# Product-key experts in a two-block model: two dense passes over the expert tables in place of gathered rows

## The chip, the cores and the metric

One core of a Trainium2 chip runs the whole program. The metric is the device time of one execution in microseconds (us); less is better.

## The reference

The input is x with 256 tokens of 1024 features, float32 throughout. A first model of two layers (recurrence, latent attention, memory attention, output projection, layer norm) is followed by one block of a second model (dilated attention and a pooling mixer, then the experts). Only the experts change:

```python
def peer_ffn(h, w_q, sub_keys, expert_u, expert_v):    # 8 heads, 2 x 128 sub-keys, top 16
    q = einsum('cd,de->ce', xc, w_q).reshape(C, 8, 2, 128)
    s = einsum('chpk,pnk->chpn', q, sub_keys)
    sv, si = top_k(s, 16)
    cand = sv[:, :, 0, :, None] + sv[:, :, 1, None, :]           # 256 sums
    cand_id = si[:, :, 0, :, None] * 128 + si[:, :, 1, None, :]
    top_v, top_pos = top_k(cand, 16)
    gate = softmax(top_v)
    u = expert_u[eid]; act = gelu(einsum('cd,chkd->chk', xc, u))
    vv = expert_v[eid]
    y = einsum('chk,chkd->cd', gate * act, vv)
```

So each token picks 8 x 16 = 128 of 16384 experts. An expert is one row of 1024 values in each of two tables of 67 MB. The block ends with x + g2 * y and an RMS norm.

## The kernel before, in words

Five engines run queues that are written out by hand. For each block a string (PE_ORDER, ACT_LAST, DVE_LAST) lists tasks, and each engine's loop at the end of its function turns a task name into instructions. Engines meet at semaphores. Nothing is planned by a scheduler: what stands behind a wait on its engine waits too.

**The tiles.** The 256 tokens are two tiles, t (0 to 127) and u (128 to 255). Weights come in units of 128 x 4096 float32 (2.1 MB) through a ring of three slots, which SP (SyncE's queue) refills as units are used up. PSUM is two tiles `pj` of 1024 columns and four banks of 512.

**The last block, up to the experts.** Scores (S), weights (P), values (Y) and the output product (O, line 775) give x; Zt and Zu turn the normed tiles (line 699) into `xT`. K0 to K3 are the units of w_q; `expert_queries` (line 1021) makes queries of them, `sub_key_scores` (line 1040, tasks E) the scores against the sub-keys, and VectorE's `route` (line 1854, tasks Rt0 to Rt7, Ru0 to Ru7) finds the top 16 of a head. K1 and K2 do not lie in the ring but in tiles that are free by then. `chosen` (line 1930) makes expert numbers of the picks with comparisons against an iota (lines 1942 to 1949).

**The experts.** Pick n = (tile, j) of 256 takes four steps. GpSimd's queue issues an indirect DMA (line 674) that gathers, for 128 tokens, one row of the joined table (u and v side by side, 2048 values) into one of 16 row slots of 1.05 MB. VectorE multiplies the u half with the token and sums it (`dots_of`, line 1993). ScalarE (`expert_weights`, lines 1407 to 1415) takes gelu, the gate, and writes a diagonal 128 x 128 matrix of the weights. TensorE multiplies that matrix with the v half, two products of 512 columns (line 1173, and 1187 for the last two picks), and sums over the picks in PSUM. A slot is gathered into again once its products are done. Tasks `D<n>` and `W<n>` say how far VectorE, ScalarE and TensorE go before the next task of another kind; picks of tile t run while queries and routes of tile u are still being made. `Ra` (line 1913) is a shortcut to the first eight picks. `Ht` and `Hu` turn the tile back into token rows for the dots.

**The end.** `end_sums` (lines 2005 to 2009) and `finish` (line 2016) add the sums to x and norm the tile; SP stores it.

Of the kernel before, what the change touches and what calls it, by code (L numbers as in the profile page):

```python
# [38 lines left out]
ROWS = PICKS * TT  # L39
GROUP = 4  # L40
N_SLOTS = 15
EARLY_SLOT, EARLY_UNTIL = N_SLOTS, 24
N_DIAG = 8
N_SPLIT = 2
# [24 lines left out]
            K0at Y3 E0t P5 Y4 Y5 Ht O1w O0v O0w K0bt W1 W2 E1t W3 W5 W6 W8 K1at K1bt W11 W14 W16 Zu W18 E2t W19 K1au W20  # L69
            W22 E3t K0au W23 W24 W25 K0bu K1bu W26 EU0 W27 W28 W29 W30 W31 Hu K20 W32 K21 W33 W35 W36 W37 W41 K22 W42  # L70
            W44 W45 K23 EU1 W46 W47 W48 W49 E4 E5 W50 K30 W51 W53 K31 W55 W56 K32 K33 W58 E6 W60 W65 W66 W67 W68 W69 E7
            W256"""]
# [4 lines left out]
ACT_LAST = """Xu BU BK BQa BQb SK S0 S1 MT S2 BV P0 P1 S3 S4 P2 S5 OMta OMtb P3 Zt K0at P4 P5 E0t Ht T1 W3 K0bt W5 W6 W7 W8  # L77
    E1t W9 OMu W10 W12 K1bt W13 W14 W15 W16 T2 W17 W18 Zu W19 W20 E2t W22 E3t W24 W25 K0bu W26 W27 W28 W29 W30 W31
    EU0 T3 K1bu W32 W33 W35 Hu W38 W39 W40 W41 W43 W44 W47 W48 W49 EU1 W50 W51 K23 E4 W52 E5 W53 W54 W56 W57 K33 W58
    W59 W60 T4 W61 W63 W64 E6 W65 W69 W70 W71 E7 W73 W78 W79 T5 W102 T6 W130 T7 W148 FN0 W256 FN1"""  # L80
# [4 lines left out]
DVE_LAST = """Xu S0 S1 S2 PL0 PL1 N0 N1 S3 N2 S4 S5 N3 N4 Y1 N5 OMt NMt Zt Ra Y5 Rt0 XP1 GT1 D1 D3 D6 OMu D7 D8 D9 Rt1 D10 D11  # L85
    D12 XP2 D14 D16 NMu D17 GT2 D19 D20 Zu D21 D23 Rt2 D24 D25 Rt3 D27 XP3 D28 D31 D34 D36 GT3 D37 D45 D47 D51 D53
    D54 D55 Rt4 D56 Rt5 XP4 D57 D60 D61 D68 Rt6 GT4 D69 D70 D72 D73 Rt7 D74 D75 D76 D78 D79 D80 XP5 GT5 D81 D83 D85
    Ru0 D88 Ru1 D92 Ru2 D96 Ru3 D100 XP6 D108 GT6 D110 Ru4 D114 Ru5 D118 Ru6 D122 Ru7 D126 XP7 D136 GT7 D140 FS0
    D156 FN0 D256 FS1 FN1"""


def pe_tasks():

    out, loads, pieces = [], 0, 0
    for text in PE_ORDER:
        tasks = []
        for task in text.split():
# [92 lines left out]
def bank_uses(l, task):  # L190

    if task in ("Xt", "Xu", "Zt", "Zu", "Ht", "Hu"):
# [5 lines left out]
    if task[0] == "E":  # L198
        return [(task,)]
    if l == B2 and task[0] == "Y":  # L200
# [31 lines left out]
def bank_index():  # L232
# [28 lines left out]
def picks_order():  # L261

    free, out, last = [], [], {}
    for n in range(ROWS):
        if n in NEW_SLOTS:
            free = list(NEW_SLOTS[n][1]) + free
        if n >= EARLY_UNTIL and EARLY_SLOT in free:
            free.remove(EARLY_SLOT)
        k = free.pop(0)
        out.append((k, last.get(k), sum(1 for q in out if q[0] == k)))  # L270
        last[k] = n
        free.append(k)
    return out


NEW_SLOTS = {0: ('', (6, 15, 2, 3, 4, 5, 7, 8)), 32: ('K1', (0, 1)), 56: ('K2', (9, 10)), 67: ('K3', (11, 12, 13)), 186: ('E7', (14,))}


def constants():
# [20 lines left out]
    for d in (4, 16):  # L300
# [13 lines left out]
        "c_iota": np.arange(16, dtype=np.float32).reshape(1, 16),  # L314
# [3 lines left out]
def build(nc, d, out):  # L318
# [9 lines left out]
    PICK = picks_order()  # L328

    with ExitStack() as ctx:  # L330
# [11 lines left out]
        more_rows = sb("more_rows", [P, 2, D_MODEL])  # L342
# [29 lines left out]
        sm = sb("sm", [P, 2, TT, T])
        pT = sb("pT", [P, 2, TT, T])
# [6 lines left out]
        flat_pair, far_pair = flat_tri[:, 0:D_MODEL], flat_tri[:, D_MODEL:].rearrange("p (h t) -> p h t", t=P)  # L380
# [21 lines left out]
        def flat(tile):  # L402
# [3 lines left out]

        shape5 = dict(t=TT, h=PEER_HEADS, two=2)
# [5 lines left out]
        top_val = flat(rstd)[:, 0:PICKS * TT].rearrange("p (t h k) -> p t h k", t=TT, h=PEER_HEADS)  # L413
        gate = flat(rstd)[:, PICKS * TT:].rearrange("p (t j) -> p t j", t=TT)
        skT = flat(sq)[:, 512:768].rearrange("p (a k) -> p a k", a=2)
        cand, cand_left = flat(sq)[:, 0:256], flat(sq)[:, 256:512]
        first_of, second_of = flat(vM)[:, 0:PICKS], flat(vM)[:, PICKS:2 * PICKS]
        id_a, id_b = flat(vM)[:, 2 * PICKS:3 * PICKS], flat(vM)[:, 3 * PICKS:4 * PICKS]
        expert = flat(vM)[:, 512:768].bitcast(u32).rearrange("p (t j) -> p t j", t=TT)
        dots = flat(vM)[:, 768:1024].rearrange("p (t j) -> p t j", t=TT)  # L420
        onehot = flat(qT).rearrange("p (j i) -> p j i", i=TOPK)

        ring_rows = [[ring[:, UNIT[B2, unit] % RING, g * 2 * D_MODEL:(g + 1) * 2 * D_MODEL] for g in range(2)]
                     for unit in ("K1", "K2", "K3")]
        flat_y = flat(yT)
        aside = [flat(b), flat_y[:, 2 * D_MODEL:]]
        spare_rows = [flat(more_rows), flat(kM)]
        row_slot = ([flat(more_rows), flat(kM), flat(qvE), flat(qM)] + ring_rows[1] + [flat(hv)]
                    + ring_rows[0] + aside + ring_rows[2] + [flat(xT), flat_y[:, 0:2 * D_MODEL], flat(kT)])
        assert len(row_slot) == N_SLOTS + 1  # L430
        diag = [far_pair[:, g, :] for g in range(4)] + [causal[:, g // 2, (g % 2) * P:(g % 2 + 1) * P] for g in range(4)]
        assert len(diag) == N_DIAG
        acts, weights_of = rope[:, 0, :], rope[:, 1, :]
        first_scores = [sm[:, i // 2, i % 2, :] for i in range(4)] + [pT[:, i // 2, i % 2, :] for i in range(4)]
# [46 lines left out]
        SPLIT_OF = {name: n for n, name in enumerate(t for t in TASKS[B2] if t in ("K0at", "K0bt", "K1bt"))}  # L481
        QUERY_OF = {name: n for n, name in enumerate(t for t in ACT_LAST.split() if t[0] == "K")}
# [30 lines left out]
        N_B2 = 5  # L513
# [5 lines left out]
        def _(sp):  # L519
# [12 lines left out]
            def weights(n):  # L532
# [41 lines left out]

            for l in range(DEPTH + 1):
                units = [name for k, name in LOADS if k == l]
                for name in units:
# [18 lines left out]
                    if name == units[3] and l == B2:  # L596
# [4 lines left out]
                        for row, c in ((row_gate1, 2), (row_gate2, 5)):  # L601
                            load(row, mod_rows[c * DC:(c + 1) * DC, :].rearrange("(o c) p -> o (c p)", o=1)
                                 .to_broadcast([P, D_MODEL]), "mod_rows_load")
                    if name == units[2] and l == B2:
# [5 lines left out]
                        load(final_g, d["final_g_2"].rearrange("(o n) -> o n", o=1).to_broadcast([P, D_MODEL]), "b2_load")  # L610
# [1555 lines left out]
```

## Time and profile before

| what | value |
|---|---|
| median of 3 runs | 1395.61 us (1394.95 to 1398.93) |
| the profiled execution: span from first to last instruction | 1393.4 us |
| TensorE busy | 1274.3 us (91%) |
| VectorE busy | 813.1 us (58%) |
| GpSimd busy | 653.1 us (47%) |
| ScalarE busy | 436.1 us (31%) |
| moved by DMA | 406.77 MB |

A busy TensorE holds the latency of its last matmuls too, so its share is more than what it computes; the distance from one matmul to the next is read from stretches in which it never waits. The span is the profiled execution's own time; the median of the runs is 2.2 us more.

### The profile page before, as it was taken

Reading aid. Unit: us, or ns where it says so; the run is one execution under the profiler, and the core shown is the slowest. Engines: PE = TensorE matmul, PEld = TensorE weight load, DVE = VectorE, ACT = ScalarE, POOL = GpSimd, SP = SyncE. Lnnn points to the kernel's source line nnn. Section 1 sums busy time; section 2 is a strip of 40 time slices with the busy share of each in tenths; the row PEclk is TensorE's granted clock in tenths of the full one; section 3 lists DMA queues with packets and bytes.
Section 4 is the critical chain, followed back from the end, with each engine's and each line's share of the span. In section 5 each row is a group of like instructions: output and inputs, shape, how many; then the busy total and the mean of one; then the engine's idle time right before and its main releaser. Section 6 shows DMA issues by size and latency. Waiting matters only on the chain.

```text
span 1393.4 us, 17185 instructions
## 1 busy us (share of the span) xinstructions
PE 1274.3 (91%) x6328; PEld 785.6 (56%) x6328; DVE 813.1 (58%) x1694; ACT 436.1 (31%) x1065; POOL 653.1 (47%) x647
## 2 busy tenths in 40 slices
PE   9999999999999999999999999989677887877886
PEld 8887686648886686549655565633232333323332
DVE  1776377441666387352357764879888654444445
ACT  1533344111334334212334433243323232222223
POOL 0556667431636667422104444455533645554540
PEclk9999999999999999999999999999998989998999
DMA  9544335546444344635449999999999999999995
GB/s 374 213 167 173 131 125 209 210 157 222 152 170 179 122 167 170 254 137 208 172 171 412 420 406 421 419 419 421 422 421 421 421 423 421 422 421 422 422 421 240
DMA packets 54061, 406.77 MB, mean 292 GB/s; under 512 B 6213, under 2 KB 8666, under 8 KB 11610
## 3 DMA queue, kind: packets, MB, share of 16 engines
q0 software_dynamic: 37184, 268.45, 46.5%
q1 hardware_dynamic: 15706, 136.18, 25.3%
q10 hardware_dynamic: 1088, 1.05, 0.3%
q8 instruction: 50, 0.82, 0.2%
q14 instruction: 33, 0.27, 0.1%
HBM read 403.53 MB, written 1.07 MB: 290 GB/s over the span
## 4 chain that ended last, share of the span: by engine, by line
PE 33%; DMA 24%; DVE 6%; ACT 3%; issue 1%; POOL 0%; DVEq 0%; ACTq 0%
DMA ring<-in_peer_uv,vM 12%; PE bank L1173 11%; PE pj L739 6%; PE pj L775 6%; DMA qM<-in_peer_uv,vM 5%; DMA xT<-in_peer_uv,vM 4%; PE pj L1036 3%; PE pj L754 3%; DMA more_rows<-in_peer_uv,vM 2%; DMA b<-in_peer_uv,vM 2%; DVE ring L1993 1%; ACT rope L1409 1%; PE bank L699 1%; DVE qM L1993 0%; PE bank L1046 0%
## 5 line engine op out<-in xcount | busy, mean ns | idle before, releaser
L739 PE MATMUL pj<-xT,ring 128*128 128x256 f32 (+1 forms) x1568 | 318.4, 363 | 0.9 <-ACT hv L1343 0.4
L739 PEld LDWEIGHTS pj<-xT,ring 128*128 128x128 f32 x1568 | 276.6, 190 | 36.5 <-issue 2.6
L674 POOL DMA_INDIRECT ring<-in_peer_uv,vM x108 | 129.8, 1202 | 124.1 <-PE bank L1173 108.2
L635 POOL TENSOR_SCALAR more_rows<-more_rows,lbt 128x256 f32<-128x256 f32 x168 | 175.7, 1046 | 16.4
L1993 DVE SCALAR_TENSOR_TENSOR ring<-ring,memT 128x1024 f32<-128x1024 f32 x110 | 133.6, 1224 | 83.9 <-DMA ring<-in_peer_uv,vM 83.2
L1407 ACT ACTIVATE rope<-vM 128x1 f32<-128x1 f32 (+2 forms) x112 | 22.6, 202 | 385.1 <-DVE ring L1993 166.1
L1173 PE MATMUL bank<-ring,causal 128*128 128x512 f32 x256 | 123.5, 629 | 20.2 <-ACT causal L1415 20.2
L775 PE MATMUL pj<-ring,yT 128*128 128x512 f32 x320 | 140.8, 594 | 0.0
L633 POOL TENSOR_SCALAR mod_part<-more_rows,lbt 128x256 f32<-128x256 f32 x24 | 22.8, 951 | 245.7 <-issue 121.3
L636 POOL TENSOR_TENSOR mod_part<-mod_part,more_rows 128x256 f32<-128x256 f32 x168 | 128.4, 765 | 14.0
L1173 PE MATMUL bank<-ring,tri 128*128 128x512 f32 x176 | 84.8, 624 | 18.5 <-ACT tri L1415 18.4
L1173 PEld LDWEIGHTS bank<-ring,causal 128*128 128x128 f32 x256 | 51.2, 203 | 88.1 <-issue 61.4
L775 PEld LDWEIGHTS pj<-ring,yT 128*128 128x128 f32 x320 | 59.8, 190 | 69.8 <-issue 69.5
L1173 PEld LDWEIGHTS bank<-ring,tri 128*128 128x128 f32 x176 | 34.0, 199 | 65.4 <-issue 38.8
L754 PE MATMUL pj<-ring,xT 128*128 128x512 f32 x160 | 70.5, 595 | 0.0
L674 POOL DMA_INDIRECT hv<-in_peer_uv,vM x21 | 25.4, 1211 | 94.8 <-DVE vM L1952 68.2
L1409 ACT ACTIVATE rope<-rope,rstd 128x1 f32<-128x1 f32 x256 | 59.6, 285 | 3.6
L1739 DVE COPY_PREDICATED tri<-level_mask,bank 128x512 f32<-128x512 uint8 x56 | 41.0, 733 | 21.4 <-PE bank L879 19.2
L754 PEld LDWEIGHTS pj<-ring,xT 128*128 128x128 f32 x160 | 29.8, 190 | 34.8 <-issue 34.4
L1305 ACT ACTIVATE big<-big 128x1024 f32<-128x1024 f32 x32 | 34.3, 1073 | 40.3 <-DVE big L1710 23.1
L1415 ACT ACTIVATE causal<-eye,rope 128x128 f32<-128x128 f32 x128 | 44.2, 393 | 1.8
L674 POOL DMA_INDIRECT qM<-in_peer_uv,vM x21 | 24.9, 1184 | 42.3 <-PE bank L1173 34.0
(386 smaller groups left out, 2053.0 us busy)
## 6 DMA issues: line engine op xcount, KB each, us to landing
ring<-in_units SPq DMA_DIRECT2D x43, 2048.0 KB, 9.5
more_rows<-in_w_ada SPq DMA_DIRECT2D x24, 1024.0 KB, 4.9
ring<-in_units SPq DMA_DIRECT2D x2, 1536.0 KB, 8.0
ring<-in_peer_uv,vM POOLq DMA_INDIRECT x108, 21.4
memT<-in_mem SPq DMA_DIRECT2D x2, 512.0 KB, 5.3
ring<-in_units SPq DMA_DIRECT2D x1, 1024.0 KB, 8.9
xT<-in_x_turned SPq DMA_DIRECT2D x1, 1024.0 KB, 10.8
x<-in_x SPq DMA_DIRECT2D x1, 1024.0 KB, 16.3
```

Of the source, the lines that this page charges most:

```text
L635: do(g.tensor_scalar(mod_w[:, c, :], mod_w[:, c, :], silu_c[:, c:c + 1], None, ALU.mult))
L636: do(g.tensor_tensor(part, part, mod_w[:, c, :], ALU.add), "mod_partial" if c == DC - 1 else None)
L674: pool.indirect_dma_start(row_slot[k], None, d["peer_uv_2"], bass.IndirectOffsetOnAxis(ap=expert[:, t, j:j + 1], axis=0))\
L739: ins = nc.tensor.matmul(pj[s][0:n, 2 * m + first:2 * m + stop], ring[:, slot, at:at + n], act[:, c, first:stop], start=(c == 0), stop=(c ...
L754: ins = nc.tensor.matmul(pj[s][:, t * COLS:(t + 1) * COLS], act[:, c, t * P:(t + 1) * P], w[:, c, :], start=(c == 0), stop=(c == DC - 1))
L775: ins = nc.tensor.matmul(pj[t][:, n * 512:(n + 1) * 512], yT[:, 4 * j + c, t * P:(t + 1) * P], w[:, c, n * 512:(n + 1) * 512], start=(firs ...
L1036: ins = nc.tensor.matmul(pj[s][:, 2 * m * P + first:2 * m * P + stop], w[c][:, m * P:(m + 1) * P], xT[:, c, first:stop], start=(c == 0), s ...
L1173: ins = nc.tensor.matmul(bank[2 * (1 - t) + half][:, :], diag[n % N_DIAG], row_slot[PICK[n][0]][:, c0:c0 + COLS], start=(j == 0), stop=(j ...
L1409: a.activation(weights_of[:, n0 + k:n0 + k + 1], acts[:, n0 + k:n0 + k + 1], ACT.Copy, scale=gate[:, t, j + k:j + k + 1]).then_inc(sem("ro ...
L1415: a.activation(diag[n % N_DIAG], eye[:, :], ACT.Copy, scale=weights_of[:, n:n + 1])\
L1739: do(v.copy_predicated(dst, mask, B), *bank_free(key))
L1993: v.scalar_tensor_tensor(out=row_slot[k][:, 0:D_MODEL], in0=row_slot[k][:, 0:D_MODEL], scalar=1.0, in1=normed[:, t, :], op0=ALU.mult, op1= ...
```

## The change

The gathered rows go away. Both tables are now read whole, for all 256 tokens, in three stages after the queries:

- **A0 to A63** (`pair_products`). A unit of the u table holds 4 of the 128 second keys for all 128 first keys. One task takes two second keys and makes 2 x 8 products of 256 columns: the dots of 256 experts with all tokens. ScalarE's gelu moves each result into `act_all`, a tile of 128 first keys x (128 second keys x 256 tokens). It lies over most of the tiles of the earlier blocks, which are now laid by hand.
- **B0 to B31** (`hot_rows`, `gated`, `batch_gates`, `batch_weights`). Tasks J0 and J1 turn the picks (first key, second key, gate) so that picks lie on partitions. For 8 tokens at a time VectorE compares them with an iota (two one-hot tiles of 128 x 1024), GpSimd multiplies one of them by the gates, TensorE makes one 128 x 128 product per token, whose entry is the gate of that pair of keys (0 where it was not picked), and VectorE multiplies it into `act_all`.
- **V0 to V31** (`value_sums`). A unit of the v table holds 4 second keys; per key, 2 tiles and 2 halves, one product of 512 columns. The first three and the last three units take the tiles apart.

Queries run tile by tile, `K<i>t` then `K<i>u`, into four halves of `pj`. `Ra`, `Ht`, `Hu`, `dots_of`, `expert_weights` and the split gathers of the last two picks are gone; `chosen` leaves first and second keys as numbers in `picks`. SP loads 64 more units. The rows of gate 2 and of the final norm are loaded late, into `xT`.

The diff, cut to its core:

```diff
-            """... K0at Y3 E0t P5 Y4 Y5 Ht O1w O0v O0w K0bt W1 W2 E1t W3 W5 W6 W8 K1at K1bt W11 ... W69 E7
-            W256"""]
+            """... K0t Y3 E0t P5 Y4 Y5 O1w O0v O0w K1t K2t E1t Zu K3t E2t K0u E3t K1u E0u K2u E1u K3u E2u A0 E3u A1 A2 A3 A4 A5
+            A6 A7 A8 A9 A10 A11 A12 A13 J0 A14 ... A29 J1 A30 A31
+            AB V0t V1t V2t V0u V1u V2u VV V29t V30t V31t V29ua V30ua V31ua V29ub V30ub V31ub"""]
...
+    both = " ".join([f"A{k}" for k in range(32, PAIRS)] + [f"B{i}" for i in range(BATCHES)])
...
-DVE_LAST = """... Y5 Rt0 XP1 GT1 D1 D3 D6 OMu D7 D8 D9 Rt1 ... D256 FS1 FN1"""
+DVE_LAST = """... Y5 Rt0 OMu NMu Zu Rt1 Rt2 Rt3 Rt4 Rt5 Rt6 Rt7
+    CEt CHt GTt Ru0 Ru1 Ru2 Ru3 Ru4 Ru5 Ru6 Ru7 CEu CHu GTu HM FS0 FN0 FS1 FN1"""
...
+            for n in range(2 * EXPERT_UNITS):
+                r = FIRST_EXPERT + n
+                ring_released(sp, r)
+                src = (d["peer_u_2"][n] if n < EXPERT_UNITS else
+                       d["peer_v_2"][:, (n - EXPERT_UNITS) * DC * COLS:(n - EXPERT_UNITS + 1) * DC * COLS])
+                load(ring[:, r % RING, :], src, f"ring_load{r % RING}")
...
-                    pool.indirect_dma_start(row_slot[k], None, d["peer_uv_2"],
-                                            bass.IndirectOffsetOnAxis(ap=expert[:, t, j:j + 1], axis=0))\
-                        .then_inc(sem(f"row_load{k}"), 16)
...
+            def gated(i):
+
+                pool.wait_ge(sem("hot_made"), 2 * (i + 1))
+                seconds = hot[:, i % 2, 1, :, :]
+                do(g.tensor_tensor(seconds, seconds, picks_turned[:, 2, i * BATCH:(i + 1) * BATCH].unsqueeze(2)
+                                   .to_broadcast([P, BATCH, NKEYS]), ALU.mult), "hot_ready")
...
+            def pair_products(task):
+
+                k, n = int(task[1:]), HALF[task]
+                slot = ring_loaded(pe, FIRST_EXPERT + k // 2)
+                half_empty(pe, n)
+                for i in range(2):
+                    for c in range(DC):
+                        at = (2 * (k % 2) + i) * D_MODEL + c * P
+                        ins = nc.tensor.matmul(half_bank[n % 4][:, i * T:(i + 1) * T], ring[:, slot, at:at + P], xT[:, c, :],
+                                               start=(c == 0), stop=(c == DC - 1))
+                last(ins, "half_filled")
+
+            def batch_gates(i):
+
+                pe.wait_ge(sem("hot_ready"), i + 1)
+                for q in range(2):
+                    key = (l, ("B", i, q))
+                    bank_empty(pe, key)
+                    for n in range(4):
+                        ins = nc.tensor.matmul(bank_of(key)[:, n * P:(n + 1) * P], hot[:, i % 2, 0, 4 * q + n, :],
+                                               hot[:, i % 2, 1, 4 * q + n, :], start=True, stop=True)
+                    last(ins)
...
+                for at in range(4):
+                    k = 4 * n + at
+                    for t in tiles:
+                        for half in halves:
...
+                            ins = nc.tensor.matmul(half_bank[2 * t + half], act_all[:, k, t * P:(t + 1) * P],
+                                                   ring[:, slot, at * D_MODEL + half * COLS:at * D_MODEL + (half + 1) * COLS],
+                                                   start=(k == 0), stop=(k == NKEYS - 1))
...
+                do(a.activation(act_all[:, 2 * k:2 * k + 2, :], half_bank[n % 4].rearrange("p (a t) -> p a t", a=2), ACT.Gelu),
...
-                    v.scalar_tensor_tensor(out=row_slot[k][:, 0:D_MODEL], in0=row_slot[k][:, 0:D_MODEL], scalar=1.0,
-                                           in1=normed[:, t, :], op0=ALU.mult, op1=ALU.mult,
-                                           accum_out=dots[:, t, j:j + 1]).then_inc(sem("dot_done"), 1)
...
+            def hot_rows(i):
+
+                if i >= 2:
+                    bank_filled(dve, (l, ("B", i - 2, 1)))
+                dve.wait_ge(sem("picks_turned"), i * BATCH // P + 1)
+                for k in range(2):
+                    v.tensor_tensor(hot[:, i % 2, k, :, :], iota[:, :].unsqueeze(1).to_broadcast([P, BATCH, NKEYS]),
+                                    picks_turned[:, k, i * BATCH:(i + 1) * BATCH].unsqueeze(2).to_broadcast([P, BATCH, NKEYS]),
+                                    ALU.is_equal).then_inc(sem("hot_made"), 1)
+
+            def batch_weights(i):
+
+                dve.wait_ge(sem("acts_kept"), PAIRS)
+                for q in range(2):
+                    key = (l, ("B", i, q))
+                    bank_filled(dve, key)
+                    t0 = i * BATCH + 4 * q
+                    weights = act_all[:, :, t0:t0 + 4]
+                    v.tensor_tensor(weights, bank_of(key)[:, :].rearrange("p (t n) -> p n t", t=4), weights,
+                                    ALU.mult).then_inc(sem(bank_free(key)[0]), 1)
...
+                elif name == "HM":
+                    hot_rows(0)
+                    for i in range(BATCHES):
+                        if i + 1 < BATCHES:
+                            hot_rows(i + 1)
+                        batch_weights(i)
...
-    arrays["peer_uv_2"] = np.concatenate([arrays.pop("peer_u_2")[0], arrays.pop("peer_v_2")[0]], axis=1)
+    arrays["peer_u_2"] = np.ascontiguousarray(arrays["peer_u_2"][0].reshape(NKEYS, EXPERT_UNITS, 4, DC, P).transpose(1, 4, 2, 3, 0)
+                                              .reshape(EXPERT_UNITS, P, DC * COLS))
+    arrays["peer_v_2"] = arrays["peer_v_2"][0].reshape(NKEYS, NKEYS * D_MODEL)
```

**How the order moves.** TensorE, before, from the last transposes ahead of the experts on (L699 with xT is Ht, L775 the last output product, L1036 queries, L1046 sub-key scores, L1173 the picks' products):

```order
L1130 MATMUL bank<-qM,qvE 64x128 x8
L699 MATMUL bank<-eye,xT 128x128 x8
L775 MATMUL pj<-ring,yT 128x512 x12
L1036 MATMUL pj<-xT,ring 128x128 x16
L1173 MATMUL bank<-hv,tri 128x512 x2
L1173 MATMUL bank<-kT,tri 128x512 x2
L1046 MATMUL bank<-sq,yT 128x128 x2
```

TensorE, changed, the same place up to K1t, and then the whole of it from K3u to the end (L756 is the output product, L1017 queries, L1029 sub-key scores, L682 transposes, L1041 `pair_products`, L1052 `batch_gates`, L1065 `value_sums`):

```order
L1151 MATMUL bank<-qM,qvE 64x128 x8
L756 MATMUL pj<-ring,yT 128x512 x12
L1017 MATMUL pj<-xT,more_rows 128x128 x4
...
L1017 MATMUL pj<-xT,ring 128x128 x32
L1029 MATMUL bank<-sq,yT 128x128 x4
L1041 MATMUL pj<-xT,ring 128x256 x16
L1029 MATMUL bank<-sq,yT 128x128 x4
L1041 MATMUL pj<-xT,ring 128x256 x208
L682 MATMUL bank<-eye,yT 128x128 x3
...
L1041 MATMUL pj<-xT,ring 128x256 x544
L1052 MATMUL bank<-hot 128x128 x256
L1065 MATMUL pj<-ring,act_all 128x512 x512
```

All queries, scores and 1024 pair products now stand ahead of the first product of the gates, and all 256 of those ahead of the first sum over values; nothing is interleaved any more but two transposes.

VectorE, before, near its end (L1993 is a dot):

```order
L1993 SCALAR_TENSOR_TENSOR xT,vM<-xT,memT 128x1024
L1993 SCALAR_TENSOR_TENSOR b,vM<-b,memT 128x1024
L1993 SCALAR_TENSOR_TENSOR yT,vM<-yT,memT 128x1024
L1603 TENSOR_SCALAR stat<-stat 128x1
L2016 TENSOR_SCALAR x<-pT,stat 128x512 x2
```

VectorE, changed, from the last gates (L1873) to the end (L1882 is `hot_rows`, L1894 `batch_weights`, L1904 and L1905 `end_sums`):

```order
L1873 TENSOR_TENSOR yT<-rstd,stat 128x128
L1882 TENSOR_TENSOR hot<-iota,vM 128x1024 x4
L1894 TENSOR_TENSOR act_all<-bank,act_all 128x128x4 x2
L1882 TENSOR_TENSOR hot<-iota,vM 128x1024 x2
L1894 TENSOR_TENSOR act_all<-bank,act_all 128x128x4 x2
...
L1882 TENSOR_TENSOR hot<-iota,vM 128x1024 x2
L1894 TENSOR_TENSOR act_all<-bank,act_all 128x128x4 x4
L1904 TENSOR_TENSOR hot<-pj,xT 128x512
```

The 256 dots are gone, and 64 comparisons and 64 small products alternate, two and two. GpSimd, which had the gathers, has 32 rows `L668 TENSOR_TENSOR hot<-hot,vM 128x1024` in their place.

## Rows read from the trace of the kernel before

**Rows 1.** The page: span, busy time by engine, GB/s in 40 equal slices, gathers' queue

```profile
span 1393.4 us, 17185 instructions
PE 1274.3 (91%) x6328; PEld 785.6 (56%) x6328; DVE 813.1 (58%) x1694; ACT 436.1 (31%) x1065; POOL 653.1 (47%) x647
...
GB/s 374 213 167 173 131 125 209 210 157 222 152 170 179 122 167 170 254 137 208 172 171 412 420 406 421 419 419 421 422 421 421 421 423 421 422 421 422 422 421 240
...
q0 software_dynamic: 37184, 268.45, 46.5%
```

**Rows 2.** Windows: start:end, length, busy of the engines, PEclk, DMA share, GB/s

```profile
500.00:600.00 100.00, 99.83 (x787) 66.05 (x786) 60.91 (x91) 30.36 (x46) 64.92 (x72) 1.00 0.52 203
1000.00:1100.00 100.00, 73.86 (x153) 30.73 (x152) 83.09 (x216) 28.98 (x96) 46.81 (x39) 0.90 1.01 421
```

**Rows 3.** Chain that ended last: start us, us, what it was

```profile
1225.62 2.00 PE bank L1173 x4
...
1227.88 24.70 DMA more_rows<-in_peer_uv,vM
...
1252.61 1.24 DVE more_rows L1993 x2
```

**Rows 4.** Timeline of TensorE: start us, us, line, operation, count, [idle before it]

```profile
725.98 1.09 PE L699 MATMUL bank<-eye,xT 128*128 128x128 f32 x8
726.91 10.47 PE L775 MATMUL pj<-ring,yT 128*128 128x512 f32 x24
737.21 3.73 PE L1036 MATMUL pj<-xT,ring 128*128 128x128 f32 x32
742.23 1.96 PE L1173 MATMUL bank<-hv,tri 128*128 128x512 f32 x4 [1.29 <-ACT tri L1415]
...
1205.76 2.84 PE L1173 MATMUL bank<-ring,causal 128*128 128x512 f32 x4 [2.81 <-ACT causal L1415]
```

**Rows 5.** Chain, TensorE never waiting: products of 256, 512, 128 and 128 columns

```profile
545.91 13.81 PE pj L739 x64
703.78 6.88 PE pj L775 x16
805.03 7.14 PE pj L1036 x64
865.88 0.89 PE bank L1046 x8
```

**Rows 6.** Timeline of VectorE: first and last row of one route; one-hot comparisons

```profile
756.84 0.48 DVE L1869 MAX8 cT<-sm 128x8 f32<-128x128 f32 x2
...
761.03 0.42 DVE L1911 FIND_INDEX8 kE<-rstd,sq 128x8 uint32<-128x256 f32 x1
...
1058.54 2.36 DVE L1942 TENSOR_TENSOR qT<-mod_part,vM 128x1024 f32<-128x1024 f32 x2
```

**Rows 7.** Groups of GpSimd by form: count, busy us and mean ns, idle before

```profile
L647 POOL TENSOR_TENSOR b<-kT,b 128x1024 f32<-128x1024 f32 x1 | 2.4, 2352 | 0.1
```

**Rows 8.** Timeline of all engines, 136 to 141: start us, us, engine, line

```profile
136.36 0.93 POOL L635 TENSOR_SCALAR more_rows<-more_rows,lbt 128x256 f32<-128x256 f32 x1
136.41 0.69 DVE L1781 SCALAR_TENSOR_TENSOR sm<-bank,causal 128x512 f32<-128x512 f32 x1 [0.21 <-DVE tri L1739]
...
137.13 0.59 ACT L1249 COPY pT<-bank 128x512 f32<-128x512 f32 x1 [2.35 <-PE bank L699]
...
139.21 0.73 POOL L636 TENSOR_TENSOR mod_part<-mod_part,more_rows 128x256 f32<-128x256 f32 x1
...
139.39 1.09 DVE L1668 TENSOR_TENSOR sm<-sm,stat 128x512 f32<-128x512 f32 x1
```

**Rows 9.** Windows as in rows 2, around a pause of TensorE

```profile
1208.00:1210.00 2.00, 2.00 (x3) 0.66 (x2) 1.12 (x2) 0.00 (x0) 1.05 (x1) 0.50 0.99 414
1210.00:1212.00 2.00, 2.00 (x6) 0.94 (x5) 1.23 (x2) 0.00 (x0) 0.57 (x1) 0.96 1.01 422
```

**Rows 10.** Chain as in rows 3, its last products

```profile
1382.45 3.45 PE bank L1187 x8
```

More of the change, by code:

```diff
@@ L68 @@
             """Xt BUt BKt Xu MT BUu BKu BQa BQb SK S0 S1 BVa S2 PL0 PL1 BVb P0 P1 S3 S4 Y0 S5 Y1 O1t P2 O0t P3 O1v Zt Y2 P4
-            K0at Y3 E0t P5 Y4 Y5 Ht O1w O0v O0w K0bt W1 W2 E1t W3 W5 W6 W8 K1at K1bt W11 W14 W16 Zu W18 E2t W19 K1au W20
-            W22 E3t K0au W23 W24 W25 K0bu K1bu W26 EU0 W27 W28 W29 W30 W31 Hu K20 W32 K21 W33 W35 W36 W37 W41 K22 W42
-            W44 W45 K23 EU1 W46 W47 W48 W49 E4 E5 W50 K30 W51 W53 K31 W55 W56 K32 K33 W58 E6 W60 W65 W66 W67 W68 W69 E7
-            W256"""]
+            K0t Y3 E0t P5 Y4 Y5 O1w O0v O0w K1t K2t E1t Zu K3t E2t K0u E3t K1u E0u K2u E1u K3u E2u A0 E3u A1 A2 A3 A4 A5
+            A6 A7 A8 A9 A10 A11 A12 A13 J0 A14 A15 A16 A17 A18 A19 A20 A21 A22 A23 A24 A25 A26 A27 A28 A29 J1 A30 A31
+            AB V0t V1t V2t V0u V1u V2u VV V29t V30t V31t V29ua V30ua V31ua V29ub V30ub V31ub"""]
 ACT_HEAD = ["MK", "X MK"]
@@ L76 @@
     Le18 HO2 HN2 HO3 HN3 LN"""
[L77 to L80, printed above, removed]
+ACT_LAST = """Xu BU BK BQa BQb SK S0 S1 MT S2 BV P0 P1 S3 S4 P2 S5 OMta OMtb P3 Zt P4 K0t E0t P5 OMua OMub K1t K2t E1t
+    Zu K3t E2t K0u E3t K1u E0u K2u E1u K3u E2u A0 E3u A1 A2 A3 A4 A5 A6 A7 A8 A9 A10 T0 A11 A12 A13 J0 A14 A15 A16 A17
+    A18 A19 A20 A21 A22 A23 A24 A25 A26 T1 A27 A28 A29 J1 A30 A31 AB FN0 FN1"""
 DVE_ORDER = """F0 N FP0 R0 R1 R2 R3 Da01 KR Da02 S0 Db01 P0 Db02 L01 S1 Da03 L02 AD Db03 Da04 F1 AD S2 Da05 L03 Da06
@@ L197, in bank_uses @@
         return [("MT",)]
-    if task[0] == "E":
+    if task[0] in "EJ":
         return [(task,)]
+    if task[0] == "B" and task[1:].isdigit():
+        return [("B", int(task[1:]), q) for q in range(2)]
     if l == B2 and task[0] == "Y":
@@ L258, in bank_index @@
     return out, uses
[L261 to L276, printed above, removed]
+HALF = {task: n for n, task in enumerate(
+    [t for t in TASKS[B2] if t[0] == "K"] + [t for t in TASKS[B2] if t[0] == "A" and t[1:].isdigit()])}
+ASIDE = [UNIT[B2, "K1"], UNIT[B2, "K2"]]
+RING_UNITS = [n for n in range(len(STREAM)) if n not in ASIDE]
+RING_AT = {n: r for r, n in enumerate(RING_UNITS)}
+FIRST_EXPERT = len(RING_UNITS)
 def constants():
@@ L419, in build @@
[L419 to L426, printed above, removed]
-        spare_rows = [flat(more_rows), flat(kM)]
@@ L428, in build @@
[L428 to L434, printed above, removed]
@@ L1019, in _, with expert_queries @@
             l = B2
-            def expert_queries(name, columns, tiles):
+            def expert_queries(task):
+                name, t = task[:2], "tu".index(task[2])
                 if name in ("K1", "K2"):
@@ L1038, in expert_queries @@
-                return ins
-            def sub_key_scores(key, ready, products):
+                n = HALF[task]
+                half_empty(pe, n)
+                after(pe, "xT_ready", l - 1, 2 * t + 5)
+                for m in range(4):
+                    for c in range(DC):
+                        ins = nc.tensor.matmul(half_bank[n % 4][:, m * P:(m + 1) * P], w[c][:, m * P:(m + 1) * P],
+                                               xT[:, c, t * P:(t + 1) * P], start=(c == 0), stop=(c == DC - 1))
```

565 lines of the change are left out of this document (208 added, 357 removed).

## The prediction, made before the changed kernel ran

> **What bounds the kernel now.** The page comes first: TensorE is busy for 91% of the span, and 268 MB, two thirds of all bytes, pass through the gathers' queue [rows 1]. The slices of GB/s then cut the kernel in two. For 21 slices, some 735 us, the DMA moves 122 to 254 GB/s after the start; for the 18 slices from there on it moves 406 to 423 [rows 1]. The windows say which limit holds in each part. From 500 to 600 TensorE is busy for 99.8 us of 100 at granted clock 1.00; from 1000 to 1100 for 73.9, while the 16 DMA engines are at 1.01 of their time [rows 2]. The chain of waits shows the cycle of the second part: two products in 2.00 us, the next gather into the slot they free, 24.7 us, a dot of 1.24 [rows 3]; gelu and diagonal on ScalarE lie between a dot and its products. So the first part is bound by TensorE, and the second, some 650 us, by 268 MB at 421 GB/s, that is 638 us. TensorE's work in it is hidden.
>
> One thing about the counts decides everything below. In the program a pick takes two products of 512 columns; in the timeline it is x4 [rows 4], and the 12 output products of O1w, O0v and O0w are x24 [rows 4]. A float32 product leaves **two records**, two passes of the array. Only transposes leave one (8 for Ht, x8) [rows 4].
>
> The prices of a record where TensorE never waits [rows 5]: 256 columns 13.81 / 64 = 0.2158 us; 512 columns 6.88 / 16 = 0.430 us; 128 columns 7.14 / 64 = 0.1116 us, and 0.89 / 8 = 0.111 us for a score.
>
> **The change, step by step.** Off goes the whole second part as it is, gathers, dots, diagonals and their slots. What takes its place has one order on TensorE, so I add it up in time.
>
> *Up to the end of the output product.* The two first models do not change on any engine. O0w ended at 737.2 [rows 4]. Ahead of it Ht goes (8 transposes, 0.93 by the distance of its start to the next row's [rows 4]), K0t has 32 products in place of 16 (+32 records, 3.57) and E0t 4 in place of 2 (+4 records, 0.45). End: 740.3.
>
> *Queries.* K1t, K2t, K3t and K0u to K3u are 7 tasks of 64 records, 7 x 7.14 = 50.0 us. Six tasks E of 8 records are 5.3, Zu 0.9. A0 begins at 796.5. Does TensorE wait here? Zu needs gate 1, two adds, the norm and ScalarE's sums for tile u; K1t, K2t and E1t give these 15 us, and a route (4.6 us from first to last row [rows 6]) ahead of them on VectorE is over by then. I take 0.
>
> *Stage A.* 64 tasks x 16 products x 2 records = 2048 x 0.2158 = **442.0 us**; E3u and the transposes J0, J1 within it are 1.6. A unit of 2.1 MB feeds 13.8 us of products, and at 421 GB/s [rows 1] it takes 5.0, so SP's loads are hidden. ScalarE has 6.9 us for each result of 512 columns; a copy of one took 0.59 [rows 8]. VectorE's routes are hidden too: 16 x 4.6 = 74 us, and for each tile 12 comparisons, multiplications and sums of 1024 elements at 1.15 (two took 2.36, of which some 0.07 is latency that overlaps what follows) [rows 6], some 16 with the rest, all over about 80 us after A0 begins, where J1 stands 30 tasks, 207 us, behind it. If that cover were gone the cost would be its excess over 207. End of A: 1240.1.
>
> *Stage B.* This is where the trace before shows no such work. Batches 0 and 1 are ready in advance, but the first `batch_weights` waits for the last gelu, and only its end lets the third pair of one-hot tiles start. Per batch: two comparisons of 128 x 1024, 2.29 [rows 6]; one GpSimd product of 128 x 1024, 2.35 [rows 7]; 16 records of 128 columns, 1.8; two small products of 128 x 512 from PSUM, 0.69 each, 1.4 [rows 8]. Whether the first two overlap decides. At 139.39 a VectorE product with both inputs in SBUF began while GpSimd's ran until 139.94, and took 1.09 us; it ended 0.54 after GpSimd's. One of the same shape with an input in PSUM took 0.69 beside a GpSimd instruction of 0.93 [rows 8]. So comparisons and gate products take turns, and the small products lie under GpSimd's. The round is 2.29 + 2.35 + 0.1 for the hand-over = 4.74 us. The ends: with no exclusion the round is VectorE's alone, 2.29 + 1.4 = 3.7; with GpSimd at the rate of its 256 columns, 4 x 0.73 = 2.92 [rows 8], it is 5.3; with the small products exposed as well, since their reads step through memory as no row before does, 6.1 or more. I take 4.74, as the rows of full width are the nearest. From the end of A: 1.1 until the first bank is filled, 1.4, 30 rounds = 142.2, and the last batch's 1.8 on TensorE: **146.5 us**. The sums over values begin at 1386.6.
>
> *Stage V.* 128 keys x 2 tiles x 2 halves = 512 products, 1024 records x 0.430 = **440.3 us**. These are as many products as the picks had, but now nothing hides them. The clock: after a pause of 2.81 us [rows 4] TensorE was at 0.50, the 1.2 GHz level, for the 2 us from 1208, and at 0.96 in the 2 us after them [rows 9]. In B it pauses 3 us in each round. Slow gates stay under VectorE's comparisons; V then starts slow, which costs about 2 us once. V0t to V2t, 20 us, cover the last small products. A unit takes 13.8 us here as well, so its transfer is hidden down to 2.1 MB / 13.8 = 152 GB/s. End: 1828.9.
>
> The rows of the v table for one unit lie 512 KB apart, 16 KB in each. The Trainium skill, "DMA: Bandwidth & Descriptors", section "Latency and other measured facts", warns of row pitches at large powers of two: 207 GB/s for copies with a pitch of 512 KiB, 103 at 4 MiB. By 207 a unit would take 10.1 us and the sum stays; by 103 it would take 20.4 and V some 190 us more (29 of them and the start). No run here shows such a load.
>
> *The end.* From the last product to the end of the span was 1393.4 - 1385.9 = 7.5 us [rows 1, 10]; the same steps follow, and tile t's lie under tile u's products. Span: 1836.4. The median of the runs was 2.2 us above the profiled span, so the forecast is **1839 us**, 32% slower. In one sum: 650 us bound by transfers are traded for 59 + 442 + 147 + 440, bound by TensorE except in B.
>
> **The rivals.**
> *The passes are one* (this ends faster). Had a product one pass, as the transposes have, A would be 221, V 220, the queries 25 and the gates no less: 1839 - 221 - 220 - 27 = 1371 us. It decides below about 0.12 us for 256 columns. For it speaks only that the order lists 1024 and 512 products; against it the x24 for 12 and the x4 for two [rows 4]. 1%.
> *No exclusion in B.* If broadcast inputs do not take the port, the round is 3.7: 31 us less, 1808. For it: no row shows two broadcast inputs. Against: rows 8. 12%.
> *A longer round.* GpSimd at 2.92, or small products that outlast GpSimd's: 5.3 to 6.1 per round, 1856 to 1880. For it: the banks are read with a step of 128 values and `act_all` in pieces of 4. [...] 22%.
> *V waits for its units.* At 122 GB/s, the lowest slice [rows 1], a unit takes 17.2 us; 29 loads one after another and the start come to 540 in place of 440: 1939. It decides at 152 GB/s. Against: gathers of scattered 8 KB rows ran at 421 [rows 1]. 5%.
> *A lower clock in A or V.* At 0.90, as in 1000 to 1100 [rows 2], they would be 98 us longer, 1937. Against: 99.8% busy at 1.00 [rows 2]. 3%.
>
> **How the numbers follow.** The forecast has 57%, its own range 1825 to 1855. A measurement can tell 0.3%, some 4 us, from no change. All cases but the first rival are far slower: slower 0.99, faster 0.01, same 0. The range takes in both ends of the round in B and ends where slow loads or a slow clock begin: 1803 to 1882.
>
> **What would show it.** TensorE's distance of 0.216 us between records in A and 0.430 in V with no idle time; A0 near 797, the first gate product of stage B's flow near 1240, V near 1387. In B, comparisons that begin while GpSimd multiplies and take over 2 us in place of 1.15, and a round of 4.7 us. DMA at about 150 GB/s in A and V. Wrong would be: TensorE waiting for `ring` in V, a round under 4 or over 6, or a granted clock below 1.00 in the middle of A.

## The result and the profile after

The changed kernel takes **1825.09 us** (median; 1824.1 to 1826.28) against 1395.66 us before: a ratio of 1.3073, 95% interval 1.3054 to 1.3091. The forecast was 1839, with 1803 to 1882; its own range, 1825 to 1855, is met only at its lower edge.

The page of the changed kernel, to be laid beside [rows 1]. Row q1 is SP's queue, which now carries the tables; the last three rows are groups of instructions (count, busy us and mean ns of one, idle time before):

```profile
span 1824.0 us, 21425 instructions
PE 1757.2 (96%) x9006; PEld 1248.1 (68%) x9006; DVE 622.6 (34%) x1219; ACT 288.9 (16%) x481; POOL 404.6 (22%) x419
...
GB/s 333 204 144 127 197 179 193 193 187 139 132 216 197 177 90 228 105 127 139 151 172 139 143 172 147 139 162 69 1 0 63 191 163 160 138 157 165 138 153 55
...
q1 hardware_dynamic: 24922, 270.46, 38.3%
L1041 PE MATMUL pj<-xT,ring 128*128 128x256 f32 x2048 | 442.7, 379 | 0.0
L1065 PE MATMUL pj<-ring,act_all 128*128 128x512 f32 x1024 | 440.6, 593 | 0.0
L668 POOL TENSOR_TENSOR hot<-hot,vM 128x1024 f32<-128x1024 f32 x32 | 61.5, 1922 | 642.6 <-DVE hot L1882 642.6
```

All bytes went from 407 to 273 MB, and the 18 slices at over 400 GB/s are gone: no slice after the first exceeds 228. TensorE went from 91% to 96% busy. Lines 1041 and 1065 show what the forecast rests on: 1024 and 512 products, 2048 and 1024 records, and no idle time ahead of any of them. In the whole stretch from 790 to 1820 TensorE's only waits are these (us in total, times, longest):

```profile
PE bank L1052 <- POOL hot L668: 50.9, 30, 3.3
```

The chain that ended last, from the last queries on (start us, us, what):

```profile
789.23 7.15 PE pj L1017 x64
796.38 0.89 PE bank L1029 x8
797.27 6.91 PE pj L1041 x32
...
1006.03 234.83 PE pj L1041 x1088
1240.85 1.80 PE bank L1052 x16
...
1251.82 2.36 DVE hot L1882 x2
1254.32 1.91 POOL hot L668
1256.27 2.06 PE bank L1052 x16
1259.62 3.07 DVE hot L1882 x2
...
1376.06 440.43 PE pj L1065 x1024
```

One can lay this beside [rows 3]. Before, the long step of each cycle was a transfer of 24.7 us; now no transfer is in the chain from 797 on. The chain is TensorE for 443.6 us, then comparisons, gate products and TensorE by turns for 135.2 us, then TensorE for 440.4.

The windows of stages A, B and V, columns as in [rows 2], the granted clock third from the end:

```profile
1000.00:1240.00 240.00, 240.00 (x1115) 211.28 (x1114) 0.00 (x0) 20.78 (x35) 0.00 (x0) 1.00 0.40 149
1260.00:1380.00 120.00, 77.11 (x440) 68.74 (x441) 106.27 (x106) 0.00 (x0) 49.74 (x27) 0.79 0.00 1
1400.00:1600.00 200.00, 200.00 (x467) 88.54 (x466) 0.00 (x0) 0.00 (x0) 0.00 (x0) 1.00 0.43 166
```

A and V hold TensorE at full clock and everything else nearly idle. In B no engine is at its end: TensorE 64%, VectorE 89% (which holds the time that its comparisons are blocked), GpSimd 41%, and DMA nothing.

The turns in B, GpSimd and then VectorE of the changed kernel (start us, us, engine, line):

```profile
1319.33 1.90 POOL L668 TENSOR_TENSOR hot<-hot,vM 128x1024 f32<-128x1024 f32 x1 [2.72 <-DVE hot L1882]
...
1323.59 1.90 POOL L668 TENSOR_TENSOR hot<-hot,vM 128x1024 f32<-128x1024 f32 x1 [2.36 <-DVE hot L1882]
```

```profile
1316.83 2.35 DVE L1882 TENSOR_TENSOR hot<-iota,vM 128x1024 f32<-128x1024 f32 x2
1319.10 1.28 DVE L1894 TENSOR_TENSOR act_all<-bank,act_all 128x512 f32<-128x512 f32 x2
1320.30 3.14 DVE L1882 TENSOR_TENSOR hot<-iota,vM 128x1024 f32<-128x1024 f32 x2
1323.37 1.27 DVE L1894 TENSOR_TENSOR act_all<-bank,act_all 128x512 f32<-128x512 f32 x2
```

The two small products, 1.28 us, run at full speed under the gate product. The two comparisons that begin at 1320.30, while it still runs until 1321.23, take 3.14 us, in place of 2.35 for the two at 1316.83, which meet no gate product. So the one that is held takes some 1.9 us, a little under the "over 2 us" that was forecast. It is the pattern of [rows 8] at full size.

### The profile page after: what moved, and what is told of

Read it like the earlier page. It is cut to its first block, busy times and chain, and to the rows that moved or that the text cites. A ratio compares the mean times of both kernels' runs of the same rounds, so it can differ in the third digit from the quotient of the medians.

```text
span 1824.0 us, 21425 instructions
## 1 busy us (share of the span) xinstructions
PE 1757.2 (96%) x9006; PEld 1248.1 (68%) x9006; DVE 622.6 (34%) x1219; ACT 288.9 (16%) x481; POOL 404.6 (22%) x419
## 4 chain that ended last, share of the span: by engine, by line
PE 69%; DVE 3%; POOL 1%; issue 1%; ACT 0%; POOLq 0%; DVEq 0%; ACTq 0%
PE pj L1041 24%; PE pj L1065 24%; PE pj L720 5%; PE pj L756 4%; PE pj L1017 3%; PE bank L1052 2%; DVE hot L1882 2%; PE pj L735 2%; POOL hot L668 1%; PE bank L682 0%; DVE act_all L1894 0%; PE bank L1029 0%; PE bank L1151 0%; PE bank L860 0%; PE bank L792 0%
## 5 line engine op out<-in xcount | busy, mean ns | idle before, releaser
L1041 PE MATMUL pj<-xT,ring 128*128 128x256 f32 x2048 | 442.7, 379 | 0.0
L1065 PE MATMUL pj<-ring,act_all 128*128 128x512 f32 x1024 | 440.6, 593 | 0.0
L1041 PEld LDWEIGHTS pj<-xT,ring 128*128 128x128 f32 x2048 | 388.8, 190 | 52.7
L1065 PEld LDWEIGHTS pj<-ring,act_all 128*128 128x128 f32 x1024 | 195.0, 191 | 245.0 <-issue 245.0
L720 PEld LDWEIGHTS pj<-xT,ring 128*128 128x128 f32 x1568 | 276.6, 190 | 36.5 <-issue 2.6
L668 POOL TENSOR_TENSOR hot<-hot,vM 128x1024 f32<-128x1024 f32 x32 | 61.5, 1922 | 642.6 <-DVE hot L1882 642.6
L1904 DVE TENSOR_TENSOR hot<-pj,xT 128x512 f32<-128x512 f32 x4 | 2.8, 693 | 432.2 <-PE pj L1065 432.1
L756 PE MATMUL pj<-ring,yT 128*128 128x512 f32 x320 | 140.9, 595 | 0.0
L1052 PE MATMUL bank<-hot 128*128 128x128 f32 x512 | 84.5, 333 | 50.9 <-POOL hot L668 50.9
L1894 DVE TENSOR_TENSOR act_all<-bank,act_all 128x512 f32<-128x512 f32 x64 | 42.3, 683 | 258.6 <-PE bank L1052 258.2
L1052 PEld LDWEIGHTS bank<-hot 128*128 128x128 f32 x512 | 77.3, 239 | 58.0 <-POOL hot L668 57.9
L756 PEld LDWEIGHTS pj<-ring,yT 128*128 128x128 f32 x320 | 59.8, 190 | 69.9 <-issue 69.7
L1381 ACT ACTIVATE act_all<-pj 128x512 f32<-128x512 f32 x64 | 38.2, 597 | 386.7 <-PE pj L1041 386.6
L1882 DVE TENSOR_TENSOR hot<-iota,vM 128x1024 f32<-128x1024 f32 x64 | 91.8, 1476 | 0.0
```

Of the source, the lines that this page charges most:

```text
L668: do(g.tensor_tensor(seconds, seconds, picks_turned[:, 2, i * BATCH:(i + 1) * BATCH].unsqueeze(2) .to_broadcast([P, BATCH, NKEYS]), ALU.mu ...
L720: ins = nc.tensor.matmul(pj[s][0:n, 2 * m + first:2 * m + stop], ring[:, slot, at:at + n], act[:, c, first:stop], start=(c == 0), stop=(c ...
L756: ins = nc.tensor.matmul(pj[t][:, n * 512:(n + 1) * 512], yT[:, 4 * j + c, t * P:(t + 1) * P], w[:, c, n * 512:(n + 1) * 512], start=(firs ...
L1041: ins = nc.tensor.matmul(half_bank[n % 4][:, i * T:(i + 1) * T], ring[:, slot, at:at + P], xT[:, c, :], start=(c == 0), stop=(c == DC - 1))
L1052: ins = nc.tensor.matmul(bank_of(key)[:, n * P:(n + 1) * P], hot[:, i % 2, 0, 4 * q + n, :], hot[:, i % 2, 1, 4 * q + n, :], start=True, s ...
L1065: ins = nc.tensor.matmul(half_bank[2 * t + half], act_all[:, k, t * P:(t + 1) * P], ring[:, slot, at * D_MODEL + half * COLS:at * D_MODEL ...
```

## The experiments

The forecast held as a whole, which says little about its terms, as errors can cancel. Each run takes one term and moves it. Theory: A and V are TensorE's two passes per float32 product, B is comparisons and gate products that exclude each other, loads are hidden, and the kernel before was bound by its gathers.

**e1, the iota in PSUM.** It takes the exclusion away and leaves the work.

```diff
+            iota_bank = half_bank[3][:, 0:NKEYS]
...
-                    v.tensor_tensor(hot[:, i % 2, k, :, :], iota[:, :].unsqueeze(1)...
+                    v.tensor_tensor(hot[:, i % 2, k, :, :], (iota_bank if i > 1 else iota[:, :]).unsqueeze(1)...
...
                         batch_weights(i)
+                        if i == 0:
+                            do(v.tensor_copy(iota_bank, iota[:, :]))
```

> The comparisons from the third batch on read the iota from PSUM (a free half of pj), so they have one input in SBUF in place of two; nothing else changes. Theory (comparisons and GpSimd's gate products exclude each other): comparisons of 2.3 us run beside the gate product of 1.9 us, the round falls from 4.33 us to VectorE's own 2.3 + 1.3 = 3.6 to 3.7, over 29 rounds 19 us less: 1806 us. Rival (the round is the chain through two one-hot buffers, GpSimd and TensorE): the round stays at 4.3, 1825 us.

Measured: 1804.78 us, 20.3 less than the changed kernel. In its timeline comparisons begin beside a running gate product and take 2.35:

```profile
1304.46 1.49 DVE L1896 TENSOR_TENSOR act_all<-bank,act_all 128x512 f32<-128x512 f32 x2
1304.69 1.90 POOL L668 TENSOR_TENSOR hot<-hot,vM 128x1024 f32<-128x1024 f32 x1 [1.57 <-DVE hot L1884]
1305.87 2.35 DVE L1884 TENSOR_TENSOR hot<-pj,vM 128x1024 f32<-128x1024 f32 x2
```

In the changed kernel two comparisons that met the gate product took 3.14. Now VectorE is the bound of B, by its own work of 2.3 + 1.3 us a round (from the fourth round on they are 3.46 and 3.68 us long by turns). What decides is one input's home, not the amount of work: all 60 comparisons with the iota in PSUM took 1.21 to 1.22 us each. The whole saving is not the exclusion's, though. TensorE was granted 1.00 here from 1260 to 1360, and the slower clock of the changed kernel costs some 4 us in B and V together, as e2 shows.

**e2, TensorE kept busy in B.**

```diff
                     last(ins)
+                if i > 1:
+                    for _ in range(4):
+                        nc.tensor.matmul(half_bank[0][:, 0:T], eye[:, :], xT[:, 0, :], start=True, stop=True)
```

> After each batch of gates from the third on TensorE runs four more float32 products of 256 columns (1.7 us) into a half of pj that nobody reads, so that its pause in the round is 0.8 us in place of 2.5. Theory (slow gates lie under the comparisons): the granted clock is 1.00 in stage B in place of 0.79, the round stays at 4.3 us, stage V no longer starts slow; 1822 to 1825 us. Rival (the 1.2 GHz clock lengthens the rounds): the rounds of 4.4 us and more fall to 4.2, up to 5 us less; below 1818 the clock would have cost more than both say.

Measured: 1824.03 us, 1.1 less. The window from 1260 to 1360, at granted clock 1.00:

```profile
1260.00:1360.00 100.00, 88.83 (x568) 76.08 (x569) 100.00 (x94) 0.00 (x0) 43.82 (x24) 1.00 0.00 1
```

At the end of its B the chain reads:

```profile
1372.96 1.73 PE pj L1057 x8
1374.69 25.32 PE pj L1068 x59
```

The sums begin at 1374.69 in place of 1376.06, behind 1.73 us of added products, so without these B would be 3.1 us shorter. Of these 0.2 us are a stage A that ended earlier; some 2.9 are B's. The median lies in the range of the theory, but the 1.1 us are no more than one kernel's runs scatter, and the 1.73 us of added products behind the last batch take back part of what the clock gave. So the rows decide: some rounds of the changed kernel do get longer under the slow clock (1319.33 - 1314.71 = 4.62 us between two gate products, where the next two are 4.26 apart). Seven of its 29 rounds take 4.43 to 4.62 us; in e2 all take 4.25 or 4.26 (29 rounds from 1245.55 to 1368.95), which is 2.2 us of the 2.9. V also takes 439.5 us in e2, and in e1, where the changed kernel needs 440.4. So by an estimate from these rows the clock of 0.79 in B costs some 3 us there and 0.9 more at the start of V.

**e3, the tiles apart in V.** Half of B moves into V, and the second table is read twice.

```diff
-            AB V0t V1t V2t V0u V1u V2u VV V29t V30t V31t V29ua V30ua V31ua V29ub V30ub V31ub"""]
+            AB VV V29ua V30ua V31ua V29ub V30ub V31ub"""]
...
+    first = " ".join(f"V{n}t" + (f" B{half + n}" if n < half else "") for n in range(EXPERT_UNITS))
...
-            for n in range(2 * EXPERT_UNITS):
+            for n in range(3 * EXPERT_UNITS):
...
```

> Stage V runs tile t over all units, then tile u over all units, which SP loads a second time (67 MB more); batches 16 to 31 of the gates stand between the units of tile t. Theory (stages add up on TensorE, loads are hidden): after A 16 rounds of 4.33 us plus 3, 440 us of sums and 16 x 1.8 of gates, 134 us in B fall to 72 + 29: 1791 us; a unit is used up in 6.9 us and loaded in 5.0. Rival (units of the second table with rows 512 KB apart load more slowly than 2.1 MB in 6.9 us, 304 GB/s): TensorE waits for the ring, at 207 GB/s 3.2 us per unit, 200 us more: near 1990 us.

Measured: 1788.23 us, 36.9 less. The chain shows a unit's 8 products and then a batch's:

```profile
1333.84 6.87 PE pj L1071 x16
1340.71 1.78 PE bank L1058 x16
1342.49 6.87 PE pj L1071 x16
1349.36 1.78 PE bank L1058 x16
```

A batch that costs a round of 4.33 us by itself costs 1.78 where TensorE has other work. And the loads keep up with a unit per 6.9 us: TensorE waited once for the ring, 1.6 us, in all of V.

**e4, one pass.** It makes real the rival that I had excluded for float32.

```diff
+            def high(rows):
+                return rows.bitcast(mybir.dt.bfloat16).rearrange("p (n two) -> p n two", two=2)[:, :, 1]
...
-                        ins = nc.tensor.matmul(half_bank[n % 4][:, i * T:(i + 1) * T], ring[:, slot, at:at + P], xT[:, c, :],
+                        ins = nc.tensor.matmul(half_bank[n % 4][:, i * T:(i + 1) * T], high(ring[:, slot, at:at + P]), high(xT[:, c, :]),
```

(and so for both operands in V)

> Stages A and V multiply the upper 16 bits of the float32 values, read as bfloat16 in place, so each product is one pass; the rest of the arithmetic stays float32, and the dots and sums have bfloat16's precision. Theory (A and V are bound by two passes of TensorE): a product of 256 columns near 0.11 us and of 512 near 0.215, A 111 us and V 110 us by TensorE alone, then both bound by their loads at 421 GB/s, 160 us each: 796 + 162 + 135 + 165 + 10 = 1268 us, faster than the kernel with gathered rows. Rival (512 KB pitch at 207 GB/s): A 160, V 325, near 1430 us. Second rival (the passes do not set the pace): 1825 us.

Measured: **1276.25 us**, 0.9146 of the kernel before (0.9130 to 0.9161). TensorE's groups and its waits:

```profile
L1041 PE MATMUL pj<-xT,ring 128*128 128x256 bf16 x1024 | 123.7, 279 | 30.2 <-DMA ring<-in_peer_u 30.2
```

```profile
PE pj L1068 <- DMA ring<-in_peer_v: 39.1, 28, 4.0
PE pj L1041 <- DMA ring<-in_peer_u: 30.2, 25, 2.6
PE bank L682 <- DVE yT L1876: 9.1, 1, 9.1
```

1024 records for 1024 products: one pass. It is also a shorter one: 0.119 us for 256 columns, where a record in float32 takes 0.2158. Now the loads bind, in A and V alike, as the windows of the two stages show:

```profile
900.00:950.00 50.00, 39.01 (x331) 30.89 (x329) 0.00 (x0) 11.94 (x20) 0.00 (x0) 1.00 1.01 429
...
1150.00:1200.00 50.00, 38.37 (x161) 14.72 (x161) 0.00 (x0) 0.00 (x0) 0.00 (x0) 1.00 1.00 427
```

427 GB/s for rows 512 KB apart, 429 for rows that follow each other. The Trainium skill, "DMA: Bandwidth & Descriptors", section "Latency and other measured facts", has 207 GB/s for copies between HBM tensors with that pitch. These loads into SBUF show nothing of it; the measurement decides.

**e5, gathers of half the bytes, in the kernel before.**

```diff
-                    pool.indirect_dma_start(row_slot[k], None, d["peer_uv_2"],
+                    pool.indirect_dma_start(row_slot[k][:, 0:D_MODEL], None, half_table,
```

> The kernel before, but each gather (save those of the last two picks, which stay as they are) fetches 4 KB per token in place of 8 KB, into the first half of its slot; the products read what the second half of the slot happens to hold, so rows and sums are not the model's. All instructions of the other engines stay. Theory (the part with gathers is bound by 268 MB at 421 GB/s): 134 MB less, and TensorE becomes the bound: 737 us, then 512 products x 2 x 0.430 = 440, queries and scores 62, 8 at the end, near 1255 to 1290 us. Rival (the cycle of dot, gelu, diagonal and products sets the pace): near 1395 us.

Measured: 1292.0 us, ratio 0.9252 (0.9236 to 0.9267). That is 2 us above the stated range, as neither engine is quite full: from 900 to 1280 TensorE is busy for 352 of 380 us and the DMA engines for 0.78 of their time at 264 GB/s. TensorE's waits there, 27.9 us in 11 pieces, are for the diagonals that ScalarE writes, so the rival's cycle of dot, gelu and diagonal has a small part in what is left; it does not set the pace, or the time would have stood near 1395. The sums of this run are not the model's.

```profile
900.00:1280.00 380.00, 352.10 (x798) 153.49 (x797) 303.39 (x700) 142.68 (x482) 215.14 (x191) 0.96 0.78 264
```

**e6, one pass in the kernel before.** The same edit as in e4 on the diagonals and value rows of lines 1173 and 1187.

> The kernel before, with the products of the picks (diagonal x values) in one pass on the upper 16 bits, read as bfloat16; all else as it was. Theory (the same saving that took a third from the dense kernel is worth nothing here, since transfers bind): 1390 to 1395 us, the few us of the last products at most. Rival (TensorE is part of the bound, as it is 80% busy): 1350 us or less.

Measured: 1393.69 us, ratio 0.9979 (0.9968 to 0.9989).

```profile
1200.00:1300.00 100.00, 34.88 (x79) 10.06 (x80) 49.35 (x80) 23.34 (x90) 43.54 (x40) 0.59 1.01 422
```

TensorE is busy for 34.9 us of 100 there, at clock 0.59, and the time stands: DMA is at 1.01. The edit that took 549 us off the dense kernel takes 3 off this one. With e5 it settles what bound the second part of the kernel before: the bytes of the gathers.

**e7, one pass, with e1 and J1 later.** In e4 TensorE waited 9.1 us for the picks of tile u, so J1 goes from behind A29 to behind A37.

```diff
-    both = " ".join([f"A{k}" for k in range(32, PAIRS)] + [f"B{i}" for i in range(BATCHES)])
+    both = " ".join([f"A{k}" for k in range(32, 38)] + ["J1"] + [f"A{k}" for k in range(38, PAIRS)] + [f"B{i}" for i in range(BATCHES)])
```

> The one-pass kernel with the iota of the comparisons in PSUM from the third batch on, and with the transposes J1 of tile u after A37 in place of A29, as TensorE waited 9.1 us for the picks of tile u there. A and V as in the one-pass kernel, in bfloat16's precision. Theory: 19 to 20 us less in B, as in float32, and 5 to 9 less in A, where the loads bind and the wait had emptied the queue: 1276 to 1248 us. Rival (rounds in B bound by something that the faster stages change): less than 15 us together, above 1260.

Measured: **1244.58 us**, ratio 0.8919 (0.8902 to 0.8937), 31.7 less than e4. The wait for the picks is gone, and A ends 7.7 us earlier (954.0 in place of 961.6). B takes 113.9 us in place of 136.5, 22.6 less and so a little more than in float32, where e1's B is 114.3 in place of 135.2. The forecast was 5 to 9 in A and 19 to 20 in B, so the median lies 3 us below the range of 1276 to 1248. Two changes are in this run; the stages keep them apart. This is the fastest kernel of the study, in bfloat16's precision for the dots and the sums; the routes, gates and everything ahead of them are float32.

**e8, half of the dots, in float32.**

```diff
-                    for c in range(DC):
+                    for c in range(4):
```

> The changed kernel in float32 with only the first four of eight chunks of features in the pair products of stage A, so the dots are sums over 512 features in place of 1024; loads, gelu and everything else stay. Theory (A is 2048 records of 0.2158 us on TensorE): 1024 records, 221 us less, 1604 us; a unit is used up in 7.0 us and loaded in 5. Rival (the loads or ScalarE's gelu set part of the pace): less is saved, at 2.1 MB in 7.6 us, its time to landing, some 20 us less of it.

Measured: 1603.5 us, 221.6 less than the changed kernel.

```profile
800.00:1015.00 215.00, 215.00 (x1005) 189.36 (x1004) 75.19 (x254) 44.31 (x71) 4.64 (x2) 1.00 0.82 300
```

TensorE has no idle time at twice the pace of loads and gelu, so neither was any part of A's time. The dots are sums over half of the features, so the result is not the model's.

## Why the prediction was right, point by point

The measured column is read from the chain of the changed kernel.

| step | forecast | measured |
|---|---|---|
| end of the output product | 740.3 | 741.0 |
| first pair product | 796.5 | 797.3 |
| end of stage A | 1240.1 | 1240.9 |
| stage B up to the first sum | 146.5 us | 135.2 us |
| stage V | 440.3 + 2 us | 440.4 us |
| from the last product to the end of the span | 7.5 us | 7.5 us |
| median of the runs less span | 2.2 us | 1.1 us |

- **The two records per product** decided the sign. e4 shows the other case: with one pass the dense kernel wins. As a rival it had 1%, rightly for float32, and its price of 1371 us left out that the loads then bind and that a pass of bfloat16 is shorter still: A's 1024 records, at 0.119 us each, are 122 us and not 221. e8 confirms A's term to 0.6 us.
- **Stage B** is where 11.3 of the 13.5 us between the sum, 1838.6, and the measured time went. The mechanism was right (e1), one size was off: the step "one GpSimd product of 128 x 1024, 2.35" measured 1.90, so the round was 4.33 (29 rounds from 1245.78 to 1371.34) and not 4.74. The row it came from [rows 7] has two full inputs, and the gate product reads one value for 128 elements. That this is what makes it cheaper is likely but not shown: no run changes it alone. I had bounded it only upwards, by 2.92; that the broadcast could be cheaper stood in no row. "Slow gates stay under VectorE's comparisons" was wrong for seven of the 29 rounds, an error of the other sign (e2).
- **The small products** were neither slow nor exposed: 683 ns each for 128 x 512, as other rows with a PSUM input. The Trainium skill ("SBUF — State Buffer", section "Door 1: The DMA port swizzle (why `[64,N]` ≈ `[32,N]`)") says of matmuls that any non-contiguous access to PSUM slows them. On VectorE nothing of the kind shows here: a contiguous read of the same size took 693 ns (line 1904), the read with a step of 128 values 683.
- **The slow start of V** was put at 2 us. The clock was 0.54 from 1376 to 1378, and V took 440.4 us as a whole, against 439.5 in e1 and e2, where it starts at 1.00: 0.9 us, so half of it. The 440.3 had rounded the price of a record up by as much. Some 3 us more of the clock's cost lie in B (e2), where the forecast had none.
- **The loads** were hidden, and by more than the bound: e3 loads a unit per 6.9 us, e4 per 4.9.
- **The bound before** was read rightly from a DMA share of 1.01 beside a TensorE of 74% (e5, e6).
- **The number** has some luck in it. The ends of the first stages came 0.7 to 0.8 us later than forecast; the round of B, V and the distance of the median from the span all came out shorter. The range held because it took in both ends of the round, and the own range by 0.1 us.

## What to carry to other kernels

Work that one engine does under another's transfers looks free, and a change that removes the transfers makes it the whole price: 440 us of products lay under the gathers, and taking out the gathers left them standing with 442 more. Count the records of an operation in the trace against its count in the program before pricing it; here one shorter pass in place of two was worth 549 us and the sign of the change. When two engines take turns, look at which inputs they read from which memory before cutting work: moving 512 bytes per partition to PSUM gave 20 us, clock included.

## What the hardware showed that I had not expected

- GpSimd multiplied 128 x 1024 by a broadcast operand in 1.90 us and by a full one in 2.35. The first gate product, which began at 990.81 beside comparisons of VectorE already under way, took 2.75: the exclusion holds whichever engine is first.
- In B of the changed kernel TensorE ran 8 products, 16 records, per round of 4.25 to 4.62 us and was granted 0.79 on average; its pauses from 1262 to 1370 were up to 2.6 us. In e1, with rounds of 3.46 and 3.67 us and pauses of 1.4 to 1.6, it was granted 1.00 from 1260 to 1360. The busy time was 60 us of 100 there and 77 of 120 in the changed kernel, but the same 16 records took 2.05 us at full clock and up to 3.8 at the slow one, so the shares can't be compared. e1 had both shorter pauses and more records per us; which of the two went with the clock these runs do not separate.
- bfloat16 read in place as every second 16-bit value of float32 data, on both operands, kept TensorE ahead of loads of 428 GB/s: a unit's 32 products of 256 columns took 3.8 us, 0.119 each.
